# Seventeen weight slots of the Conformer's first product as three matmuls of split parts

## The chip, the cores and the metric

The kernel runs on one core of one Trainium2 chip. The metric is the device time of one execution in microseconds, less is better. Before the change it is 2429.86 us, the median of three runs (2427.54 to 2431.71).

## The reference

Two transformer-like blocks in fp32 follow each other for one sequence of 256 tokens of width 2048. The change lies in the first mixer, the Conformer's convolution, and its first product `h @ w_in`:

```python
def conformer_conv(h, w_in, b_in, dw, dw_b, ln_g, ln_b, w_out, b_out):
    u = h @ w_in + b_in
    val, gate = jnp.split(u, 2, axis=-1)
    u = val * jax.nn.sigmoid(gate)
    u = causal_dwconv(u, dw) + dw_b
    u = jax.nn.silu(layernorm(u, ln_g, ln_b))
    return u @ w_out + b_out
```

h is the normed input (256 x 2048), w_in is 2048 x 4096, and the convolution has 31 taps per channel. Behind it come a squared-relu MLP, a second block (gated delta rule and block attention, cross attention to a memory of 256 rows, a gated FFN) and a last norm. The keys and values of that memory are computed early, right behind the Conformer's first product.

## The kernel before

Activations lie transposed: 128 channels on the partitions, 16 channel tiles, 256 tokens along the free axis. All weights stream from DRAM in slots of 128x1024 fp32 (two channel tiles of 512 columns), one after another in one list, into a ring of four raw buffers `w_raw`. SyncE issues the loads (`sp_load`, L472).

There are two ways to multiply. From the product behind the layer norm on, fp32 is emulated: ScalarE rounds a slot to its high part in fp32r (`act_hi`, L499), VectorE subtracts it from the raw slot to get the low part (`dve_lo`, L508), and TensorE adds hi x hi, hi x lo and lo x hi (`pe_product`, L524, with its matmuls at L553). Before that, in the first 80 slots, it is plain fp32 straight from the raw buffer (`pe_plain_product`, L558): 64 slots of `cc_in` (eight products b = 0 to 7 of eight slots each; a product gives 256 gate and 256 value channels) and 8 slots each of the memory's keys and values. Each plain fp32 matmul shows as two records in the trace.

While TensorE runs product b+1, ScalarE takes the sigmoid of the gates of b (L1065), VectorE multiplies the values with it (glu, L1205) and convolves: for each of two channel tiles of a b a first tap (L1162) and 30 more (L1165), each waiting for the one before it on its tile. Two PSUM accumulators alternate between the products, so product b+2 waits for the glu of b. The glu has three buffers, the gate two. The mean of the layer norm is a set of small matmuls over the convolved tiles (`add_to_mean`, L947); its last part stands on TensorE between keys and values and waits for the last tap. GpSimd clears a few columns at the start and then has nothing to do until the second block.

Each engine has its own program in a fixed order, written out by hand. A helper calls `act_hi` and `dve_lo` once for each slot that TensorE passes, four slots ahead; at the last slot of a product the gates (ScalarE) or the glu (VectorE) stand in front of that call. Other short work (the memory norm's root, the convolution's steps) is put between slots as threads that advance one step per slot.

The first four split slots (80 to 83) are loaded into buffers of their own, `w_first`, that lie over `w_lo`, while slots 64 to 67 are being requested. `w_hi` lies over `mem_in`, the memory's rows.

Of the kernel before, what the change touches and what calls it, by code (L numbers as in the profile page):

```python
# [7 lines left out]
F32 = mybir.dt.float32  # L8
# [5 lines left out]
P = 128  # L14
T = 256
# [188 lines left out]
def side_by_side(both):  # L204
    return Operand(both[:, :, 0, :], both[:, :, 1, :], both)
# [31 lines left out]
STRIP = P // CT  # L237
EARLY = KT // SLOT_K * 2
WARM = 5
WIDE_K = SLOT_K * COLS // PAIR  # L240


class Kernel:
# [40 lines left out]
    def buffers(self):  # L284
        self.x = self.sbuf("x_residual", [P, KT, T])
        with ExitStack() as early:
            self.normed = self.sbuf("h_plain", [P, KT, T], F32, early)
        self.h = side_by_side(self.sbuf("h_operand", [P, KT, 2, T], F32R))
        self.mem_k = self.sbuf("mem_k", [P, NX, T])
        self.mem_v = self.sbuf("mem_v", [P, TT, NX * HD])  # L290
# [18 lines left out]
        with ExitStack() as first:  # L309
            sb = lambda name, shape, dt=F32: self.sbuf(name, shape, dt, first)  # L310
            with ExitStack() as early:
                self.mem_scaled, self.squares = (self.sbuf(n, [P, KT, T], F32, early) for n in ("mem_scaled", "first_squares"))
            with ExitStack() as early:
                self.sbuf("below_conv_hi", [P, KT, T], F32R, early)
                conv_hi = self.sbuf("conv_hi", [P, KT, T], F32R, early)
            hidden = sb("mlp_hidden", [P, KT, 2, T], F32R)
            self.u = sb("conv_out", [P, KT, T])
            self.gate_buf = [sb(f"gate{i}", [P, PT, T]) for i in range(2)]
            self.glu_buf = [sb(f"glu{i}", [P, PT, CONV_K - 1 + T]) for i in range(3)]
            self.mean, self.mem_col = sb("mean", [P, T]), sb("mem_column", [P, TT])  # L320
            self.conv_operand = Operand(conv_hi, sb("conv_lo", [P, KT, T], F32R))
        first, second = (b.rearrange("p k t -> p (k t)") for b in self.tmp_buf)
        self.hot, self.neg, self.rel = first[0:BUCKETS, 0:BIAS_W], second[0:NM, 0:BIAS_W], second[0:BUCKETS, COLS:COLS + NM]
        self.inputs = [self.sbuf(f"heads{g}", [P, 4, CT, T]) for g in range(2)]
# [58 lines left out]
    def plan(self):  # L383
        d = self.dram
        self.parts, self.slots, self.on_pool, self.order = [], {}, [], {}

        def product(key, name, col, pool, k0=0, n=D):
            first = len(self.parts)
            for r in range(k0, k0 + n, SLOT_K * P):
                self.parts.append([d[name][r:r + SLOT_K * P, col:col + COLS].rearrange("(k p) n -> p k n", p=P)])  # L390
            self.slots[key] = range(first, len(self.parts))
            self.on_pool += [pool and i % pool == 0 for i in self.slots[key]]

        def wide(key, name, col, k0=0, n=D, in_turn=False):
            steps, rows = [], range(k0, k0 + n, WIDE_K * P)
            for s, half in [(s, half) for s in range(len(rows)) for half in range(2)] if in_turn else [
                    (s, half) for half in range(2) for s in range(len(rows))]:
                steps.append((half, s, len(self.parts)))
                c = col + half * PAIR
                self.parts.append([d[name][rows[s]:rows[s] + WIDE_K * P, c:c + PAIR].rearrange("(k p) n -> p k n", p=P)])  # L400
                self.on_pool.append(False)
            self.order[key] = [(half, s, i, s == len(rows) - 1) for half, s, i in steps]

        for b in range(D // PAIR):
            first = len(self.parts)
            for r in range(0, D, SLOT_K * P):
                w = d["cc_w_in"][r:r + SLOT_K * P, :].rearrange("(k p) n -> p k n", p=P)
                self.parts.append([w[:, :, D + b * PAIR:D + (b + 1) * PAIR], w[:, :, b * PAIR:(b + 1) * PAIR]])
            self.slots["cc_in", b] = range(first, len(self.parts))
            self.on_pool += [False] * len(self.slots["cc_in", b])  # L410
        product(("keys",), "w_xkv_2", 0, 0)
        product(("values",), "w_xkv_2", COLS, 0)
        self.n_plain = len(self.parts)
        self.early = range(self.n_plain, self.n_plain + SPLIT)
        for b in range(CT):
            product(("cc_out", b), "cc_w_out", b * COLS, 0)
        for kind, c in up_down(N_MLP):
            if kind == "up":
                for b in range(MLP_CHUNK // COLS):
                    wide(("w1", c, b), "mlp_w1", c * MLP_CHUNK + b * COLS, in_turn=c == b == 0)  # L420
            else:
                for b in range(CT):
                    wide(("w2", c, b), "mlp_w2", b * COLS, c * MLP_CHUNK, MLP_CHUNK)
        for g in range(2):
            for part in range(3):
                product(("w_in", part, g), "w_in_2", part * GW + g * COLS, 0)
        for b in MOBA_BLOCKS:
            product(("moba", b), "w_in_2", 4 * GW + 2 * NG + b * COLS, 0)
        for g in range(2):
            product(("w_in", 3, g), "w_in_2", 3 * GW + g * COLS, 0)  # L430
        for half, b in W_OUT_ORDER:
            product(("w_out", half, b), "w_out_2", b * COLS, 0, half * GW, GW)
        wide(("xq",), "w_xq_2", 0)
        for b, half in XO_ORDER:
            product(("xo", b, half), "w_xo_2", b * COLS, 0, half * PAIR, PAIR)
        for kind, c in FFN_ORDER:
            if kind == "up":
                wide(("gate", c), "w_gate_2", c * COLS, in_turn=c == 0)
                wide(("up", c), "w_up_2", c * COLS)
            else:  # L440
                for b in range(CT):
                    wide(("ffn_down", c, b), "w_down_2", b * COLS, c * 2 * COLS, len(chunks_of(c)) * COLS)
        self.n_slots = len(self.parts)

    def lo_done(self, i):
        return (self.pool_done if self.on_pool[i] else self.dve_done).at("w_lo", i)


def spread_row(row, n):
    return row.unsqueeze(1).broadcast_to([P, n, T])  # L450
# [14 lines left out]
def cut(t):  # L465
    return slice(t * P, (t + 1) * P)
# [5 lines left out]
def sp_load(k, sp, i):  # L472
    if i >= k.n_slots:
        return
    if i in k.early:
        return
    if i >= RAW:
        if i - RAW < k.n_plain:
            sp.wait_ge(*k.pe_done.at("used", i - RAW))
        elif i - RAW in k.early:  # L480
            sp.wait_ge(*k.pe_done.at("used", i - 2 * RAW))
        else:
            sp.wait_ge(*k.lo_done(i - RAW))
    parts = k.parts[i]
    w = k.w_raw_wide[i % RAW] if parts[0].shape[1] == WIDE_K else k.w_raw[i % RAW]
    width = w.shape[2] // len(parts)
    for n, part in enumerate(parts):
        sp.dma_start(w[:, :, n * width:(n + 1) * width], part).then_inc(*k.w_landed[i % RAW].mark(i))


def sp_load_early(k, sp, i):
    sp.dma_start(k.w_first[i % SPLIT], k.parts[i][0]).then_inc(*k.w_early[i % SPLIT].mark(i))


# [2 lines left out]


def act_hi(k, act, i):  # L499
    if i >= k.n_slots or i < k.n_plain:  # L500
        return
    act.wait_ge(*(k.w_early[i % SPLIT].at(i) if i in k.early else k.w_landed[i % RAW].at(i)))
    if i >= k.n_plain + SPLIT:
        act.wait_ge(*k.pe_done.at("used", i - SPLIT))
    act.activation(k.w_hi[i % SPLIT], raw_of(k, i), ACT.Copy).then_inc(*k.act_done.mark("w_hi", i))  # L505


def dve_lo(k, dve, i):  # L508
    if i >= k.n_slots or i < k.n_plain or k.on_pool[i]:
        return  # L510
    dve.wait_ge(*k.act_done.at("w_hi", i))
    dve.tensor_tensor(k.w_lo[i % SPLIT], raw_of(k, i), k.w_hi[i % SPLIT].bitcast(F32), ALU.subtract).then_inc(  # L512
        *k.dve_done.mark("w_lo", i))


def pool_lo(k, pool, i):
# [43 lines left out]
def pe_plain_product(k, pe, key, x, ready, tokens_out=False, every=CT):  # L560
    psum, free = k.acc.take(key)
    for f in free:
        pe.wait_ge(*f)
    for s, i in enumerate(k.slots[key]):
        w = k.w_raw[i % RAW]
        pe.wait_ge(*k.w_landed[i % RAW].at(i))
        for part in range(TT if tokens_out else CT):
# [13 lines left out]
        if i == k.slots[key][-1]:  # L581
            k.pe_done.note(*key)
        k.pe_beside.step()


def pe_wide_product(k, pe, key, x, ready, k_tiles=range(KT), every=CT):
# [301 lines left out]
def pool_conformer(k, pool):  # L888
    for i, v in enumerate([1e-6, 1e-5, 128e-6]):
        pool.memset(k.eps[:, i:i + 1], v).then_inc(*k.pool_done.mark("eps"))  # L890
    for buf in k.glu_buf:
        pool.memset(buf[:, :, 0:CONV_K - 1], 0.0).then_inc(*k.pool_done.mark("glu padded"))


def pe_sum_of_squares(k, pe, norm, n_before):
# [104 lines left out]
def act_conformer(k, act):  # L1000
# [66 lines left out]
    for b in range(D // PAIR):  # L1067
        act_product(k, act, ("cc_in", b), lambda: gates(b))
        if b == 0:
            k.act_beside.start(mem_norm())  # L1070
        if b == 5:
            act.wait_ge(*k.dve_done.at("bias rows"))
# [54 lines left out]
def dve_conformer(k, dve):  # L1127
# [26 lines left out]
    def convolve(b):  # L1154
        src = k.glu.at(b)
        dve.wait_ge(*k.dve_done.at("glu", b))
        for j in range(CONV_K):
            for t in range(PT):
                n = b * PT + t
                out, tap, w = k.u[:, n, :], src[:, t, j:j + T], k.col("cc_dw", n * CONV_K + j)  # L1160
                if j == 0:
                    dve.tensor_scalar(out, tap, w, k.col("cc_dw_b", n), ALU.mult, ALU.add).then_inc(*k.dve_done.mark("tap", t, b, j))  # L1162
                else:
                    dve.wait_ge(*k.dve_done.at("tap", t, b, j - 1))
                    dve.scalar_tensor_tensor(out=out, in0=tap, scalar=w, in1=out, op0=ALU.mult, op1=ALU.add).then_inc(  # L1165
# [1824 lines left out]
```

## Time and profile before

| | |
|---|---|
| median of three runs | 2429.86 us (2427.54 to 2431.71) |
| span of the profiled execution | 2427.0 us, 2.9 us under the median |
| TensorE busy | 2395.6 us, 99% |
| VectorE busy | 1658.4 us, 68% |
| ScalarE busy | 1122.0 us, 46% |
| GpSimd busy | 59.5 us, 2% |
| traffic with HBM | 176 GB/s over the span |
| end of the eight first products | 230.8 us |
| end of keys, and of values | 259.3 us, 288.9 us |

The span goes from the first to the last instruction of one profiled execution; the time that this execution took as a whole is not given beside it. Busy shares are averages over stages that differ much. A matmul's duration reaches over the start of the next, so durations don't add up: the distance from start to start is what one costs.

### The profile page before, as it was taken

The numbers are of one execution on the slowest core, as the hardware profiler recorded it, in microseconds if no ns is written. First come the engines' busy times: TensorE is split into PE (matmuls) and PEld (weight loads), VectorE is DVE, ScalarE is ACT, GpSimd is POOL, SyncE is SP. The second block draws the span as 40 slices with busy tenths as digits, with TensorE's granted clock in tenths as the row PEclk, the third lists the DMA queues.
The fourth block names the chain that finished last, engine by engine and source line by source line (L and its number), as shares of the span: only waits on it lengthen the run. The fifth ranks groups of instructions, "written<-read, shape, count | busy, mean of one in ns | idle before, by whom it ended". The sixth has DMA issues, their size and how long they took to land. (4 is left out here: it accounts for less than half of the span.)

```text
span 2427.0 us, 39495 instructions
## 1 busy us (share of the span) xinstructions
PE 2395.6 (99%) x16354; PEld 2126.6 (88%) x16354; DVE 1658.4 (68%) x2310; ACT 1122.0 (46%) x1510; POOL 59.5 (2%) x47
## 2 busy tenths in 40 slices
PE   9999999999999999999999999999999999999998
PEld 8888699888888888889997997998888888888886
DVE  5999756666666666678766455567766767667677
ACT  4000445544544544555637356556544444444444
POOL 0000000000000000000000000000100101000000
PEclk9999999999999999999999999999999999999999
DMA  7446456666666666655444455454666666666663
GB/s 248 152 148 208 146 179 196 191 190 191 190 185 193 190 188 192 190 183 164 141 126 123 123 165 147 157 190 150 191 191 184 194 187 189 189 187 191 186 192 125
DMA packets 379762, 427.96 MB, mean 176 GB/s; under 512 B 16537, under 2 KB 328129, under 8 KB 379585
## 3 DMA queue, kind: packets, MB, share of 16 engines
q1 hardware_dynamic: 374464, 421.58, 56.4%
q10 hardware_dynamic: 5120, 3.86, 0.5%
q8 instruction: 131, 2.15, 0.4%
q14 instruction: 47, 0.38, 0.0%
HBM read 423.27 MB, written 3.67 MB: 176 GB/s over the span
## 5 line engine op out<-in xcount | busy, mean ns | idle before, releaser
L512 DVE TENSOR_TENSOR w_lo<-w_raw,w_hi 128x1024 fp32r<-128x1024 f32 x708 | 868.4, 1229 | 543.8 <-ACT w_hi L505 543.1
L505 ACT ACTIVATE w_hi<-w_raw 128x1024 fp32r<-128x1024 f32 x708 | 747.4, 1058 | 817.9 <-PE product L606 578.6
L604 PE MATMUL product<-h_operand,w_hi 128*128 128x512 f32 x2496 | 867.6, 393 | 0.8 <-DVE x_residual L808 0.8
L606 PE MATMUL product<-h_operand,w_lo 128*128 128x256 f32 x2496 | 696.7, 279 | 0.0
L604 PEld LDWEIGHTS product<-h_operand,w_hi 128*128 128x128 f32 x2496 | 467.8, 187 | 105.9 <-DVE x_residual L808 1.1
L606 PEld LDWEIGHTS product<-h_operand,w_lo 128*128 128x128 f32 x2496 | 471.5, 189 | 0.1
L604 PE MATMUL product<-mlp_hidden,w_hi 128*128 128x512 f32 x1024 | 355.3, 394 | 0.0
L606 PE MATMUL product<-mlp_hidden,w_lo 128*128 128x256 f32 x1024 | 284.0, 277 | 0.0
L604 PE MATMUL product<-mid_operand,w_hi 128*128 128x512 f32 x704 | 248.9, 397 | 0.0
L553 PE MATMUL product<-h_operand,w_hi 128*128 128x256 f32 x1280 | 239.2, 288 | 0.3 <-DVE w_lo L512 0.3
L604 PEld LDWEIGHTS product<-mlp_hidden,w_hi 128*128 128x128 f32 x1024 | 192.3, 188 | 44.7
L578 PE MATMUL product<-h_plain,w_raw 128*128 128x256 f32 x1024 | 222.7, 380 | 0.5 <-DMA w_raw<-in_cc_w_in 0.5
L578 PEld LDWEIGHTS product<-h_plain,w_raw 128*128 128x128 f32 x1024 | 194.5, 190 | 28.5 <-DMA w_raw<-in_cc_w_in 1.3
L553 PEld LDWEIGHTS product<-h_operand,w_hi 128*128 128x128 f32 x1280 | 200.3, 193 | 4.0 <-issue 1.1
L606 PE MATMUL product<-mid_operand,w_lo 128*128 128x256 f32 x704 | 198.4, 282 | 0.0
L606 PEld LDWEIGHTS product<-mlp_hidden,w_lo 128*128 128x128 f32 x1024 | 192.4, 188 | 0.0
L1165 DVE SCALAR_TENSOR_TENSOR conv_out<-glu,feature_columns,conv_out 128x256 f32<-128x256 f32 x480 | 190.8, 474 | 0.0
L661 DVE TENSOR_TENSOR x_residual<-x_residual,product 128x512 f32<-128x512 f32 x224 | 153.8, 687 | 43.2 <-PE product L606 39.4
L553 PE MATMUL product<-h_operand,w_lo 128*128 128x256 f32 x640 | 181.7, 284 | 0.0
L604 PEld LDWEIGHTS product<-mid_operand,w_hi 128*128 128x128 f32 x704 | 132.2, 188 | 32.4
L606 PEld LDWEIGHTS product<-mid_operand,w_lo 128*128 128x128 f32 x704 | 133.2, 189 | 0.0
L553 PEld LDWEIGHTS product<-h_operand,w_lo 128*128 128x128 f32 x640 | 123.4, 193 | 0.0
(333 smaller groups left out, 2242.3 us busy)
## 6 DMA issues: line engine op xcount, KB each, us to landing
w_raw<-in_mlp_w SPq DMA_DIRECT2D x256, 512.0 KB, 3.9
w_raw<-in_w_in SPq DMA_DIRECT2D x112, 512.0 KB, 3.7
w_raw<-in_w_gate SPq DMA_DIRECT2D x88, 512.0 KB, 3.6
w_raw<-in_w_up SPq DMA_DIRECT2D x88, 512.0 KB, 4.1
w_raw<-in_w_down SPq DMA_DIRECT2D x88, 512.0 KB, 4.5
w_raw<-in_cc_w_in SPq DMA_DIRECT2D x128, 256.0 KB, 2.9
w_raw<-in_w_out SPq DMA_DIRECT2D x32, 512.0 KB, 3.7
w_raw<-in_cc_w_out SPq DMA_DIRECT2D x28, 512.0 KB, 4.6
```

Of the source, the lines that this page charges most:

```text
L505: act.activation(k.w_hi[i % SPLIT], raw_of(k, i), ACT.Copy).then_inc(*k.act_done.mark("w_hi", i))
L512: dve.tensor_tensor(k.w_lo[i % SPLIT], raw_of(k, i), k.w_hi[i % SPLIT].bitcast(F32), ALU.subtract).then_inc(*k.dve_done.mark("w_lo", i))
L553: done = pe.matmul(out, stationary, moving, start=first and opens, stop=final, skip_group_check=True)
L578: done = pe.matmul(psum[:, part * T:(part + 1) * T], w[:, kk, cut(part)], x[:, kt, :], start=first and part % 2 == 0, stop=final, skip_gro ...
L604: pe.matmul(out, hi[:, kk, n], x.both[:, kt].rearrange("p a t -> p (a t)"), start=s == 0 and kk == 0, stop=False, skip_group_check=True)
L606: done = pe.matmul(out[:, 0:T], lo[:, kk, n], x.hi[:, kt, :], start=False, stop=last and kk == WIDE_K - 1, skip_group_check=True)
L661: dve.tensor_tensor(x, x, row, ALU.add).then_inc(*k.dve_done.mark("added", *key, half))
L1165: dve.scalar_tensor_tensor(out=out, in0=tap, scalar=w, in1=out, op0=ALU.mult, op1=ALU.add).then_inc(*k.dve_done.mark("tap", t, b, j))
```

## The change

Slots 1, 4 and 6 of the products b = 2 to 7 are taken from the plain path, except slot 62, which a range at the end of the plan clears again: slots 17, 20, 22, 25, 28, 30, 33, 36, 38, 41, 44, 46, 49, 52, 54, 57 and 60. Each gets a high part by ScalarE and a low part by GpSimd, in the rings `w_hi` and `w_lo` that are otherwise unused at that time, and 24 matmuls in place of the 8 plain ones. The activations are split once: high part by ScalarE after the gates of b=0, low part by GpSimd into the buffer of `conv_lo`. The raw buffer of a split slot is free for the next load when GpSimd has subtracted. The first tap of the convolution becomes a scalar_tensor_tensor with the bias column broadcast.

```diff
+SPLIT_FROM, SPLIT_STEPS = 2, (1, 4, 6)
...
-            self.on_pool += [False] * len(self.slots["cc_in", b])
+            self.on_pool += [s in SPLIT_STEPS and b >= SPLIT_FROM for s in range(len(self.slots["cc_in", b]))]
...
+        for i in range(self.n_plain - EARLY - RAW + 1, self.n_plain):
+            self.on_pool[i] = False
+        self.in_parts = [i for i in range(self.n_plain) if self.on_pool[i]]
...
+    def split_of(self, i):
+        n = self.in_parts.index(i)
+        return self.w_hi[n % SPLIT], self.w_lo[n % SPLIT], self.in_parts[n - SPLIT] if n >= SPLIT else None
...
-        if i - RAW < k.n_plain:
+        if i - RAW in k.in_parts:
+            sp.wait_ge(*k.lo_done(i - RAW))
+        elif i - RAW < k.n_plain:
             sp.wait_ge(*k.pe_done.at("used", i - RAW))
...
 def sp_load_early(k, sp, i):
+    sp.wait_ge(*k.pe_done.at("used", k.in_parts[-1]))
...
 def act_hi(k, act, i):
+    if i in k.in_parts:
+        hi, _, before = k.split_of(i)
+        act.wait_ge(*k.w_landed[i % RAW].at(i))
+        act.wait_ge(*(k.act_done.at("squares", "mem_norm", CT - 1) if before is None else k.pe_done.at("used", before)))
+        act.activation(hi, k.w_raw[i % RAW], ACT.Copy).then_inc(*k.act_done.mark("w_hi", i))
...
+    if i in k.early:
+        act.wait_ge(*k.pe_done.at("used", k.in_parts[-1]))
...
+def pool_lo_of_plain(k, pool, i):
+    hi, lo, before = k.split_of(i)
+    pool.wait_ge(*k.act_done.at("w_hi", i))
+    if before is not None:
+        pool.wait_ge(*k.pe_done.at("used", before))
+    pool.tensor_tensor(lo, k.w_raw[i % RAW], hi.bitcast(F32), ALU.subtract).then_inc(*k.pool_done.mark("w_lo", i))
...
+def pe_slot_in_parts(k, pe, psum, s, i):
...
+    pe.wait_ge(*k.pool_done.at("normed lo", s * SLOT_K // CT))
+    pe.wait_ge(*k.act_done.at("w_hi", i))
+    for part, kk in tiles:
+        add(hi, k.normed_hi, part, kk)
+        add(hi, k.normed_lo, part, kk)
+    pe.wait_ge(*k.lo_done(i))
+    for part, kk in tiles:
+        done = add(lo, k.normed_hi, part, kk)
+    return done
...
+    for g in range(CT):
+        part = slice(g * CT, (g + 1) * CT)
+        pool.wait_ge(*k.act_done.at("normed hi", g))
+        pool.tensor_tensor(k.normed_lo[:, part, :], k.normed[:, part, :], k.normed_hi[:, part, :].bitcast(F32),
+                           ALU.subtract).then_inc(*k.pool_done.mark("normed lo", g))
+    for i in k.in_parts:
+        pool_lo_of_plain(k, pool, i)
...
+            for g in range(CT):
+                act.wait_ge(*k.dve_done.at("normed", g))
+                act.activation(k.normed_hi[:, g * CT:(g + 1) * CT, :], k.normed[:, g * CT:(g + 1) * CT, :], ACT.Copy).then_inc(
+                    *k.act_done.mark("normed hi", g))
...
-                    dve.tensor_scalar(out, tap, w, k.col("cc_dw_b", n), ALU.mult, ALU.add).then_inc(*k.dve_done.mark("tap", t, b, j))
+                    dve.scalar_tensor_tensor(out=out, in0=tap, scalar=w, in1=k.col("cc_dw_b", n).broadcast_to([P, T]), op0=ALU.mult,
+                                             op1=ALU.add).then_inc(*k.dve_done.mark("tap", t, b, j))
```

## Rows read from the trace of the kernel before

**Rows 1.** The page: busy time, and the tenths in 40 slices of 60.7 us.
```profile
PE 2395.6 (99%) x16354; PEld 2126.6 (88%) x16354; DVE 1658.4 (68%) x2310; ACT 1122.0 (46%) x1510; POOL 59.5 (2%) x47
...
PE   9999999999999999999999999999999999999998
...
DVE  5999756666666666678766455567766767667677
```

**Rows 2.** Timeline of TensorE: start, duration, line, operation, out<-in, count, idle before.
```profile
72.71 55.42 PE L578 MATMUL product<-h_plain,w_raw 128*128 128x256 f32 x256
127.96 0.38 PE L931 MATMUL small<-masks,rows 128*128 128x128 f32 x2
...
259.28 0.64 PE L952 MATMUL small<-conv_out,masks 128*32 128x256 f32 x8
```

**Rows 3.** Timeline of ScalarE, the gates of b=1.
```profile
62.12 0.84 ACT L1065 ACTIVATE gate<-product,feature_columns 128x256 f32<-128x256 f32 x2 [21.94 <-PE product L578]
```

**Rows 4.** Timeline of VectorE, 70 to 258 us, and the page's row of its taps.
```profile
70.42 0.87 DVE L1205 SCALAR_TENSOR_TENSOR glu<-product,feature_columns,gate 128x256 f32<-128x256 f32 x2
71.33 0.73 DVE L1162 TENSOR_SCALAR conv_out<-glu,feature_columns 128x256 f32<-128x256 f32 x2
71.98 23.83 DVE L1165 SCALAR_TENSOR_TENSOR conv_out<-glu,feature_columns,conv_out 128x256 f32<-128x256 f32 x60
95.74 0.86 DVE L1205 SCALAR_TENSOR_TENSOR glu<-product,feature_columns,gate 128x256 f32<-128x256 f32 x2
...
122.61 0.86 DVE L1205 SCALAR_TENSOR_TENSOR glu<-product,feature_columns,gate 128x256 f32<-128x256 f32 x2
...
175.98 0.88 DVE L1205 SCALAR_TENSOR_TENSOR glu<-product,feature_columns,gate 128x256 f32<-128x256 f32 x2 [2.21 <-ACT gate L1065]
...
203.61 0.88 DVE L1205 SCALAR_TENSOR_TENSOR glu<-product,feature_columns,gate 128x256 f32<-128x256 f32 x2 [2.23 <-ACT gate L1065]
...
232.00 0.88 DVE L1205 SCALAR_TENSOR_TENSOR glu<-product,feature_columns,gate 128x256 f32<-128x256 f32 x2 [2.99 <-ACT gate L1065]
...
233.56 23.83 DVE L1165 SCALAR_TENSOR_TENSOR conv_out<-glu,feature_columns,conv_out 128x256 f32<-128x256 f32 x60
...
L1165 DVE SCALAR_TENSOR_TENSOR conv_out<-glu,feature_columns,conv_out 128x256 f32<-128x256 f32 x480 | 190.8, 474 | 0.0
```

**Rows 5.** Timeline of TensorE, the first product behind the layer norm.
```profile
288.35 0.68 PE L553 MATMUL product<-conv_hi,w_hi 128*128 128x256 f32 x1
288.87 0.28 PE L553 MATMUL product<-conv_lo,w_hi 128*128 128x256 f32 x1
...
309.01 0.28 PE L553 MATMUL product<-conv_hi,w_lo 128*128 128x256 f32 x1
```

**Rows 6.** ScalarE's line L505, its timeline, the page's DMA issues, a window of 217 us.
```profile
L505 ACT ACTIVATE w_hi<-w_raw x708: 1037/1061/1240, 293.4 to 2401.1; 128x1024 fp32r<-128x1024 f32 x177
...
36.92 1.04 ACT L1015 ACTIVATE first_squares<-mem_in 128x1024 f32<-128x1024 f32 x1
...
w_raw<-in_cc_w_in SPq DMA_DIRECT2D x128, 256.0 KB, 2.9
...
40.00:257.00 217.00, 217.00 (x1019) 188.83 (x1018) 208.79 (x519) 13.15 (x23) 0.00 (x0) 1.00 0.52 166
```

**Rows 7.** Timelines of GpSimd and VectorE where both have work, and GpSimd alone.
```profile
1744.20 2.27 POOL L2875 TENSOR_TENSOR heads<-heads,rows 128x512 f32<-128x512 f32 x1 [30.72 <-ACT heads L2714]
...
1744.09 1.22 DVE L512 TENSOR_TENSOR w_lo<-w_raw,w_hi 128x1024 fp32r<-128x1024 f32 x1
1745.23 1.72 DVE L2793 TENSOR_SCALAR heads<-heads,feature_columns 128x256 f32<-128x256 f32 x2
...
1755.35 2.26 POOL L2875 TENSOR_TENSOR heads<-heads,rows 128x512 f32<-128x512 f32 x1 [8.88 <-ACT heads L2714]
...
1757.08 1.62 DVE L512 TENSOR_TENSOR w_lo<-w_raw,w_hi 128x1024 fp32r<-128x1024 f32 x1 [0.61 <-ACT w_hi L505]
...
1709.15 1.30 POOL L2875 TENSOR_TENSOR heads<-heads,rows 128x512 f32<-128x512 f32 x1 [52.09 <-ACT heads L2714]
...
1341.68 0.74 POOL L2051 TENSOR_TENSOR squares<-squares,masks 128x256 f32<-128x256 f32 x1 [10.69 <-PE small L1680]
```

**Rows 8.** Timeline of VectorE, the first low part of the layer norm's output.
```profile
280.41 0.69 DVE L1258 TENSOR_TENSOR conv_lo<-conv_out,conv_hi 128x512 fp32r<-128x512 f32 x1
```

**Rows 9.** TensorE's restart, then windows: PE, PEld, DVE, ACT, POOL busy, PEclk, DMA share, GB/s.
```profile
1517.29 1.08 PE L2069 MATMUL small<-masks,heads 128*128 128x128 f32 x4 [3.14 <-DVE heads L2202]
...
1518.00:1519.00 1.00, 1.00 (x7) 1.00 (x5) 0.27 (x1) 0.59 (x1) 0.00 (x0) 0.50 0.00 0
...
1520.00:1521.00 1.00, 1.00 (x6) 0.80 (x5) 0.00 (x0) 1.00 (x1) 0.00 (x0) 0.89 0.86 295
```

More of the change, by code:

```diff
@@ L287, in buffers @@
             self.normed = self.sbuf("h_plain", [P, KT, T], F32, early)
+            self.normed_hi = self.sbuf("h_plain_hi", [P, KT, T], F32R, early)
         self.h = side_by_side(self.sbuf("h_operand", [P, KT, 2, T], F32R))
@@ L320, in buffers @@
             self.mean, self.mem_col = sb("mean", [P, T]), sb("mem_column", [P, TT])
-            self.conv_operand = Operand(conv_hi, sb("conv_lo", [P, KT, T], F32R))
+            self.normed_lo = sb("conv_lo", [P, KT, T], F32R)
+            self.conv_operand = Operand(conv_hi, self.normed_lo)
         first, second = (b.rearrange("p k t -> p (k t)") for b in self.tmp_buf)
@@ L564, in pe_plain_product @@
     for s, i in enumerate(k.slots[key]):
+        if i in k.in_parts:
+            done = pe_slot_in_parts(k, pe, psum, s, i)
+            done.then_inc(*k.pe_done.mark("used", i))
+            k.pe_beside.step()
+            continue
         w = k.w_raw[i % RAW]
@@ L583, in pe_plain_product, with add @@
         k.pe_beside.step()
+def pe_slot_in_parts(k, pe, psum, s, i):
+    hi, lo, _ = k.split_of(i)
+    tiles = [(part, kk) for part in range(CT) for kk in range(SLOT_K)]
+    def add(w, x, part, kk):
+        return pe.matmul(psum[:, part * T:(part + 1) * T], w[:, kk, cut(part)], x[:, s * SLOT_K + kk, :], start=False, stop=False,
+                         skip_group_check=True)
+    pe.wait_ge(*k.pool_done.at("normed lo", s * SLOT_K // CT))
[7 more added lines that the diff above has]
+    return done
 def pe_wide_product(k, pe, key, x, ready, k_tiles=range(KT), every=CT):
```

## The prediction

> **What bounds the kernel now.** I read the page first. TensorE is busy for 99% of the span and VectorE for 68%, but slices 2 to 4 of the tenths (61 to 243 us) show both at 9: in the Conformer's first product VectorE is as full as TensorE [rows 1]. So I asked for the timeline of each engine in the first 300 us. TensorE goes from plain fp32 matmul to plain fp32 matmul without a gap; between 72.71 us and 127.96 us it runs 256 records, which are 16 slots, so a slot takes 55.25 / 16 = 3.45 us and a product b of eight slots 27.6 us [rows 2]. VectorE convolves behind it. A tap goes every 23.83 / 60 = 0.397 us, and a whole b takes 95.74 - 70.42 = 25.3 us. VectorE starts late (glu of b=1 at 70.42, though its gate was done at 62.96 [rows 3]), catches up by about 2.3 us per b, and first waits at b=5. It waits 2.21, 2.23 and 2.99 us in b=5, 6 and 7, 7.4 us together, and that is all the spare time that it has until the last tap at 233.56 + 23.83 = 257.4 us [rows 4]. TensorE needs that last tap at 259.28 us, for the mean of the layer norm [rows 2]. Two clocks thus run to that point, and VectorE's is late by nature: 1.9 us of slack behind it, 7.4 us in it.
>
> **What TensorE gains.** Slots 1, 4 and 6 of b = 2 to 7 are split, except slot 62, which the range at the end of the plan clears: 6 x 3 - 1 = 17. A plain slot is 8 tiles of two records, 3.45 us. A split one is 24 matmuls of 256 columns. The order hi with hi, hi with lo, lo with hi is in the trace as the product behind the layer norm, where 172 starts lie between 288.87 and 309.01 us, 0.1171 us each [rows 5], so 24 of them take 2.81 us. A slot saves 0.64 us, 17 save 10.9 us, all on TensorE's own path. TensorE alone would be at the mean at 248.4 instead of 259.3 us.
>
> **What feeds the split.** ScalarE gets 17 conversions of weights and four of the activations, 1.06 us each, 22.3 us [rows 6], beside the 13.2 us that it is busy in the 217 us between 40 and 257 us. A raw slot is asked for when the slot four before it is done, lands 2.9 us later [rows 6], and TensorE arrives three slots, 10.4 us, after the request. 10.4 - 2.9 - 1.1 leaves 6.4 us for GpSimd's part, more than twice what it takes below, so I cost ScalarE and the new waits of SyncE at nothing. If this cover is gone (slot 4 of a b, whose conversion is queued behind the gates of the b before, and these behind VectorE's glu of two b before), TensorE waits for as long as ScalarE was held; queued there too are the root of the memory norm and the later conversions. Gates of b need glu of b-2, as TensorE's accumulator of b does, so the hold adds nothing to that wait. SyncE's load into a raw buffer of a split slot waits for GpSimd's subtraction and not for TensorE: earlier, nothing lost. The early loads behind the last split slot (60) stand in a queue that has already waited for slot 60: nothing. w_hi lies over the memory rows; ScalarE has finished their squares at 37.96 us [rows 6], well before slot 17.
>
> **What GpSimd takes from VectorE.** GpSimd gets 4 + 17 = 21 subtractions of 128x1024, and VectorE's taps, each reading glu and conv_out from SBUF, run beside all of them. The trace has no such pair, so I take the nearest rows [rows 7]. At 1744.20 a GpSimd multiply of 128x512 begins 0.11 us after the start of a VectorE subtraction, which ends at 1745.31; it ends at 1746.47, 1.16 us after that subtraction. Alone the same multiply takes 1.30 us, so it did nothing until VectorE had finished. VectorE's next pair, two tensor_scalar of 128x256, was ready at 1745.23 and took 1.72 us; a like pair with GpSimd idle takes 0.73 us [rows 4]. VectorE lost 0.99 of the 1.16 us. At 1757.08 a weight subtraction falls into the rest of a GpSimd multiply (over at 1757.61), takes 1.62 us, not 1.22, and ends 1.09 us behind the multiply: 0.13 us of its start were hidden. So the two engines exclude each other for a whole instruction, and GpSimd came first at the change of instruction even where VectorE had the next one ready. For 1024 elements: alone 128x256 takes 0.74 us, 128x512 1.30 us, so 2.19 ns an element, and the hold is 1.16 + 512 x 2.19 ns = 2.28 us, the loss 2.28 - 0.15 = 2.13 us. The bounds for one subtraction: 0, if taps don't collide; 2.5 us, if nothing of its start is hidden. A gain is excluded, since nothing is taken off VectorE. I take 2.13, because the weight subtraction (two SBUF inputs, fp32, one element per cycle) is the same kind of reader as a tap. 21 x 2.13 = 44.7 us.
>
> The Trainium skill, "SBUF — State Buffer", section "SBUF: two separate sides", says the port pair shared by VectorE and GpSimd is an exclusive lock, which a VectorE operation with two SBUF inputs takes too against a GpSimd operation that reads SBUF, and the loser blocks fully. By that rule taps collide like the weight subtraction, which no row here shows for a tap; if only VectorE's faster modes took the lock, the sum would be the first rival's. The same skill, "GPSIMD Engine Reference", section "Performance versus the Vector engine", gives 4497 ns for 2048 elements; by it, as an estimate, the hold is 2.25 us and the sum 0.6 us lower.
>
> **VectorE's own edit.** The first tap becomes a scalar_tensor_tensor. A pair of the old ones is followed after 0.65 us (71.33 to 71.98), of the new after 2 x 0.397 = 0.79 us [rows 4]: 0.15 us for each of 8 b, 1.2 us.
>
> **The sum.** VectorE never waits now: last tap at 257.4 - 7.4 + 44.7 + 1.2 = 295.9 us. On the way TensorE is held too. Products alternate between two accumulators, so product b+2 starts only when glu of b is done. Glu of b=3, at 122.61 before, comes after some ten subtractions at about 144 us, when TensorE (114 us at the end of b=3) has just finished or is about to finish b=4; from there TensorE follows VectorE at 25.5 + 3 x 2.1 = about 32 us per b, so each b has idle stretches of some 6 us. These are inside VectorE's time. It ends the keys near 275 us and waits for the last tap until 295.9 instead of 259.3: +36.6 us. Behind it nothing is tight: in the layer norm the first low part is ready at 281.1 for TensorE's 288.35 [rows 5, 8], and both move together. A wait of some 20 us brings TensorE's clock down. The only long waits of the trace show it: idle from 1514.1 to 1517.3, granted clock 0.50 (1.2 GHz of 2.4) until 1520, 0.89 in the next slice [rows 9]; some 3.3 us at half speed lose 1.7 us. Only the last wait's counts, as the others lie in VectorE's shadow. 2427.0 + 36.6 + 1.7 = 2465.3 us of span. The span is 2.9 us under the median of 2429.86; with the same 2.9 the median becomes 2468.2 us.
>
> **Rivals.**
> First, faster: the taps don't collide, or hardly. For it: no row shows a tap beside GpSimd being held. Against: 1744.20 and 1757.08 [rows 7]. VectorE then ends at 257.4 - 7.4 + 1.2 = 251.2 us, later than TensorE's 248.4, so of the 10.9 us only 259.3 - 251.2 = 8.1 are gained: 2421.8 us. This is the other sign, and it turns at (8.1 / 21) = 0.39 us lost per subtraction: below this the kernel is faster, above it slower.
> Second, worse: taps follow each other so closely that VectorE keeps the port, and GpSimd gets it only where VectorE has a gap or reads PSUM (glu). For it: taps overlap by 0.08 us (0.474 long, 0.397 apart [rows 4]), and the only pair that showed who comes next was not two taps. Against: there too the next instruction had started before the other ended, and GpSimd got in. Then slot 17 waits for five subtractions until VectorE runs dry at 96 us, ends at about 106, and b=2 at 125 instead of 88; each further b waits for VectorE at its slot 4 and takes 40 us. Last tap: 125 + 5 x 40 + 25 = 350 us, +91: about 2523 us.
> Third: the subtractions collide, but in part (handover cheap, a third to two thirds of the hold lost): 0.8 to 1.5 us each, last tap at 268 to 283, 2439 to 2455 us.
>
> **Chances and range.** Forecast 0.67; taps not colliding 0.17; in part 0.09; GpSimd starved 0.05; anything else 0.02. The forecast's own range is 2459 to 2478 us: 1.9 to 2.5 us for each subtraction gives -5 to +8, TensorE's clock and a delayed row of the memory norm the rest. Two in ten must not be left out, so the range goes down to the first rival: 2420 to 2478. A change of 0.2%, 4.9 us, is about what can be told from none. Faster: the first rival and a little of the third at its cheap end, 0.18. Same: 0.04, losses near 0.39 us. Slower: 0.78.
>
> **What would show it.** TensorE: the split slots at 0.117 us per matmul, waits for VectorE's glu from b=5 on, and one of some 20 us before the strips of the mean. VectorE: no idle time at the glu of b=5 to 7, taps beside GpSimd of 2.5 us and more, their mean raised from 474 to about 570 ns. GpSimd: 21 subtractions of 2.3 to 2.7 us. ScalarE: 17 more conversions and no wait of TensorE for them. I am wrong if taps beside GpSimd keep their 474 ns, or if TensorE's longest new wait is for GpSimd.

## The result: 2493.0 us, 2.6% slower

The changed kernel takes 2492.97 us (median of four runs, 2491.29 to 2493.68) against 2430.30 us before; the ratio is 1.0259, 95% interval 1.0240 to 1.0278. Slower was forecast, but at 2468 us with 2478 as the upper end. The measured rise of 62.7 us is 1.6 times the forecast's 38.3.

First the page of the changed kernel: busy time, then the tenths of its 40 slices (62.3 us each).

```profile
PE 2401.1 (96%) x16490; PEld 2138.9 (86%) x16490; DVE 1686.0 (68%) x2310; ACT 1143.6 (46%) x1531; POOL 198.4 (8%) x68
...
PE   9886899999999999999999999899999999999998
...
DVE  5996676666666666678766455467776766767677
...
POOL 2556200000000000000000000000010100000000
PEclk9987899999999999999999999999999999999999
```

Beside [rows 1], TensorE has lost its nines in slices 2 to 5, and VectorE its nine in slice 4 (in 5 it goes from 7 to 6): both engines that filled this stage now idle in it. TensorE's granted clock falls in slices 3 to 5. GpSimd is busy for 198 us, not the 108 that its 59.5 and 21 subtractions of 2.3 us make. The rest of the span looks as before.

Who TensorE waited for from 60 to 290 us (us in all, times, longest):

```profile
PE product L624 <- POOL w_lo L541: 54.5, 7, 13.7
PE product L624 <- ACT w_hi L517: 3.3, 1, 3.3
```

L624 is the split slot's matmuls, L541 GpSimd's subtraction. Before the change TensorE waited for nothing here. Now 57.8 us are waits for a split slot's parts, nearly all for the low part of the weights. So GpSimd's timeline comes next. In it the duration of an instruction counts from its issue, and a wait for the SBUF port that GpSimd shares with VectorE is inside it:

```profile
41.10 9.83 POOL L947 TENSOR_TENSOR conv_lo<-h_plain,h_plain_hi 128x1024 fp32r<-128x1024 f32 x4 [39.97 <-ACT h_plain_hi L1130]
59.86 6.95 POOL L541 TENSOR_TENSOR w_lo<-w_raw,w_hi 128x1024 fp32r<-128x1024 f32 x1 [8.93 <-ACT w_hi L517]
70.16 2.34 POOL L541 TENSOR_TENSOR w_lo<-w_raw,w_hi 128x1024 fp32r<-128x1024 f32 x1 [3.34 <-ACT w_hi L517]
77.72 7.58 POOL L541 TENSOR_TENSOR w_lo<-w_raw,w_hi 128x1024 fp32r<-128x1024 f32 x1 [5.23 <-ACT w_hi L517]
86.72 2.66 POOL L541 TENSOR_TENSOR w_lo<-w_raw,w_hi 128x1024 fp32r<-128x1024 f32 x1 [1.42 <-ACT w_hi L517]
99.40 17.15 POOL L541 TENSOR_TENSOR w_lo<-w_raw,w_hi 128x1024 fp32r<-128x1024 f32 x2 [10.02 <-ACT w_hi L517]
...
155.84 20.33 POOL L541 TENSOR_TENSOR w_lo<-w_raw,w_hi 128x1024 fp32r<-128x1024 f32 x2 [8.43 <-ACT w_hi L517]
185.42 19.77 POOL L541 TENSOR_TENSOR w_lo<-w_raw,w_hi 128x1024 fp32r<-128x1024 f32 x2 [9.25 <-ACT w_hi L517]
217.40 22.84 POOL L541 TENSOR_TENSOR w_lo<-w_raw,w_hi 128x1024 fp32r<-128x1024 f32 x2 [12.21 <-ACT w_hi L517]
250.03 2.35 POOL L541 TENSOR_TENSOR w_lo<-w_raw,w_hi 128x1024 fp32r<-128x1024 f32 x1 [9.79 <-ACT w_hi L517]
268.92 11.58 POOL L541 TENSOR_TENSOR w_lo<-w_raw,w_hi 128x1024 fp32r<-128x1024 f32 x1 [16.54 <-ACT w_hi L517]
```

Let in at once, a subtraction takes 2.34 or 2.35 us (70.16, 250.03). Of the rows with two, the first alone takes 14.6 (99.40), 17.8 (155.84), 17.4 (185.42) and 20.5 us (217.40). The reader should compare their ends with VectorE's timeline, which answers to [rows 4]:

```profile
142.62 0.87 DVE L1268 SCALAR_TENSOR_TENSOR glu<-product,feature_columns,gate 128x256 f32<-128x256 f32 x2
143.53 4.17 DVE L1224 SCALAR_TENSOR_TENSOR conv_out<-glu,feature_columns 128x256 f32<-128x256 f32 x2
147.62 23.84 DVE L1228 SCALAR_TENSOR_TENSOR conv_out<-glu,feature_columns,conv_out 128x256 f32<-128x256 f32 x60
171.38 0.87 DVE L1268 SCALAR_TENSOR_TENSOR glu<-product,feature_columns,gate 128x256 f32<-128x256 f32 x2
172.28 4.17 DVE L1224 SCALAR_TENSOR_TENSOR conv_out<-glu,feature_columns 128x256 f32<-128x256 f32 x2
...
210.17 0.88 DVE L1268 SCALAR_TENSOR_TENSOR glu<-product,feature_columns,gate 128x256 f32<-128x256 f32 x2 [9.51 <-ACT gate L1123]
211.08 0.88 DVE L1224 SCALAR_TENSOR_TENSOR conv_out<-glu,feature_columns 128x256 f32<-128x256 f32 x2
211.88 23.83 DVE L1228 SCALAR_TENSOR_TENSOR conv_out<-glu,feature_columns,conv_out 128x256 f32<-128x256 f32 x60
252.75 0.88 DVE L1268 SCALAR_TENSOR_TENSOR glu<-product,feature_columns,gate 128x256 f32<-128x256 f32 x2 [17.03 <-ACT gate L1123]
...
295.14 0.88 DVE L1268 SCALAR_TENSOR_TENSOR glu<-product,feature_columns,gate 128x256 f32<-128x256 f32 x2 [16.84 <-ACT gate L1123]
296.05 0.88 DVE L1224 SCALAR_TENSOR_TENSOR conv_out<-glu,feature_columns 128x256 f32<-128x256 f32 x2
296.85 23.84 DVE L1228 SCALAR_TENSOR_TENSOR conv_out<-glu,feature_columns,conv_out 128x256 f32<-128x256 f32 x60
```

Sixty taps from 147.62 take 23.84 us, the 23.83 of [rows 4] and not a hold among them, though GpSimd asked at 155.84. It got the port at the glu of 171.38, and both its subtractions were over by 176.17: the two first taps behind that glu took 4.17 us instead of 0.88. TensorE had been waiting for the first subtraction. In b=5 to 7 the glus stand 42.6 and 42.4 us apart. VectorE finishes its taps, GpSimd gets in, TensorE finishes the product, and only then may the next glu begin; so VectorE waits 17 us for TensorE after TensorE has waited for VectorE's taps to end.

Both engines' accounts close. VectorE's last tap ends at 320.7 us, before at 257.4: 63.3 later. Its idle time grew from 7.4 to 43.4 us, +36.0; the other 27.3 are 1.2 of its own edit and 26.1 of holds. TensorE reaches the mean at 322.43 instead of 259.28 [rows 2]: +63.1, of which 57.8 are waits and -10.9 the saving. I put the rest, 16.2 us, down to its clock, which each of the long waits brings down. In windows of 1 us from 60 to 330, TensorE's busy time times the missing share of the granted clock comes to 14.5 us, so some 2 us of it stay unexplained. The split slot at 269 us starts its matmuls 0.21 us apart, the one at 256 us 0.12 us:

```profile
256.00 0.28 PE L624 MATMUL product<-h_plain_hi,w_hi 128*128 128x256 f32 x1
256.11 0.28 PE L624 MATMUL product<-conv_lo,w_hi 128*128 128x256 f32 x1
...
269.55 0.41 PE L624 MATMUL product<-h_plain_hi,w_hi 128*128 128x256 f32 x1
269.76 0.41 PE L624 MATMUL product<-conv_lo,w_hi 128*128 128x256 f32 x1
```

### The profile page after: what moved, and what is told of

Its sections match the earlier page's. It is cut to its first block and busy times, and to the rows that moved or that the text cites. A ratio compares the mean times of both kernels' runs of the same rounds, so it can differ in the third digit from the quotient of the medians.

```text
span 2490.0 us, 39849 instructions
## 1 busy us (share of the span) xinstructions
PE 2401.1 (96%) x16490; PEld 2138.9 (86%) x16490; DVE 1686.0 (68%) x2310; ACT 1143.6 (46%) x1531; POOL 198.4 (8%) x68
## 5 line engine op out<-in xcount | busy, mean ns | idle before, releaser
L657 PEld LDWEIGHTS product<-h_operand,w_lo 128*128 128x128 f32 x2496 | 472.5, 189 | 0.1
L655 PEld LDWEIGHTS product<-mlp_hidden,w_hi 128*128 128x128 f32 x1024 | 191.7, 187 | 41.5
L1228 DVE SCALAR_TENSOR_TENSOR conv_out<-glu,feature_columns,conv_out 128x256 f32<-128x256 f32 x480 | 199.8, 494 | 0.0
L611 PE MATMUL product<-h_plain,w_raw 128*128 128x256 f32 x752 | 173.6, 391 | 0.5 <-DMA w_raw<-in_cc_w_in 0.5
L611 PEld LDWEIGHTS product<-h_plain,w_raw 128*128 128x128 f32 x752 | 147.1, 198 | 22.8 <-DMA w_raw<-in_cc_w_in 1.3
L541 POOL TENSOR_TENSOR w_lo<-w_raw,w_hi 128x1024 fp32r<-128x1024 f32 x17 | 129.1, 7604 | 100.5 <-ACT w_hi L517 100.5
```

The source lines that it names most:

```text
L541: pool.tensor_tensor(lo, k.w_raw[i % RAW], hi.bitcast(F32), ALU.subtract).then_inc(*k.pool_done.mark("w_lo", i))
L611: done = pe.matmul(psum[:, part * T:(part + 1) * T], w[:, kk, cut(part)], x[:, kt, :], start=first and part % 2 == 0, stop=final, skip_gro ...
L655: pe.matmul(out, hi[:, kk, n], x.both[:, kt].rearrange("p a t -> p (a t)"), start=s == 0 and kk == 0, stop=False, skip_group_check=True)
L657: done = pe.matmul(out[:, 0:T], lo[:, kk, n], x.hi[:, kt, :], start=False, stop=last and kk == WIDE_K - 1, skip_group_check=True)
```

## The experiments

Theory A: a subtraction that asks for the port while taps run is not let in until the taps pause; TensorE waits for it, then VectorE for TensorE. Theory B: the holds of VectorE are the cost and are dearer than forecast. Each experiment edits the changed kernel. The ratios are against the kernel before on the same chip.

**A pause in the taps.**
```diff
             if j % 4 == 3:
+                dve.wait_ge(*k.dve_done.at("tap", PT - 1, b, j))
                 yield
```


> VectorE waits for its last tap after every fourth pair of taps, so that there is an instant without a tap every 3.3 us; everything else is as in the changed kernel. Theory A (a subtraction that asks for the port while taps run is not let in until the taps pause; TensorE waits for it, then VectorE for TensorE): TensorE's waits for GpSimd, 54.5 us, go almost wholly, VectorE keeps its loss of about 2.1 us for each of 21 subtractions, 2458 to 2474 us. Theory B (the 2493 us come from what VectorE is held, a hold is dearer than forecast): no gain, 2493 to 2500 us, since more subtractions now cut into taps.

2475.7 us, ratio 1.0194 (1.0175 to 1.0213): 17 us faster than the changed kernel by the medians, 2 us above A's range (2458 to 2474), and far from B. Here is GpSimd, then VectorE's last b, then TensorE's waits:

```profile
59.81 2.37 POOL L541 TENSOR_TENSOR w_lo<-w_raw,w_hi 128x1024 fp32r<-128x1024 f32 x1 [8.81 <-ACT w_hi L517]
70.23 2.44 POOL L541 TENSOR_TENSOR w_lo<-w_raw,w_hi 128x1024 fp32r<-128x1024 f32 x1 [8.05 <-ACT w_hi L517]
...
198.55 3.82 POOL L541 TENSOR_TENSOR w_lo<-w_raw,w_hi 128x1024 fp32r<-128x1024 f32 x1 [15.98 <-ACT w_hi L517]
...
275.00 24.71 DVE L1228 SCALAR_TENSOR_TENSOR conv_out<-glu,feature_columns,conv_out 128x256 f32<-128x256 f32 x60
...
PE small L1010 <- DVE conv_out L1228: 23.3, 1, 23.3
PE product L611 <- DVE glu L1269: 18.4, 4, 7.2
```

All 17 subtractions now take 2.34 to 3.82 us, and TensorE waits for none of them. It waits as the forecast had it: some 5 us for the glu in the later b and 23.3 us for the last tap. That tap ends at 299.7. The pause itself costs 24.71 - 23.83 = 0.88 us in a b, 7.0 in eight; without it the end would be at 292.7, where the forecast has 295.9. That is 41.5 us above the 251.2 without GpSimd, 1.98 us for each of 21.

**The low parts by VectorE.** All 21 subtractions move to VectorE, as steps between taps. Shown is the part for the weights.
```diff
...
 def dve_lo(k, dve, i):
+    if i in k.in_parts:
+        hi, lo, before = k.split_of(i)
+        dve.wait_ge(*k.act_done.at("w_hi", i))
+        if before is not None:
+            dve.wait_ge(*k.pe_done.at("used", before))
+        dve.tensor_tensor(lo, k.w_raw[i % RAW], hi.bitcast(F32), ALU.subtract).then_inc(*k.dve_done.mark("w_lo", i))
...
```


> All 21 subtractions by VectorE instead of GpSimd, as steps between its taps; TensorE as in the changed kernel. Theory A and B alike: no port to share, VectorE pays 21 x 1.14 us = 24 us and has 7.4 us idle, last tap at 257.4 - 7.4 + 1.2 + 24 = 275 us, 2444 to 2450 us, if TensorE's low parts come in time. Rival: VectorE is so late with its steps that TensorE waits at split slots in turn: over 2455 us.

2446.6 us, ratio 1.0081 (1.0053 to 1.0109). The last tap ends at 275.6, the sum said 275. TensorE waits 13.1 us for low parts in small pieces; these lie inside VectorE's time. The same split without the shared port costs 46 us less than the changed kernel, and still more than no split.

**No subtraction at all.** The split slots' matmuls read the high parts twice, low parts are left out, GpSimd has nothing to do, and the next load into a split slot's raw buffer waits for ScalarE's conversion alone.
```diff
...
-        add(hi, k.normed_lo, part, kk)
-    pe.wait_ge(*k.lo_done(i))
+        add(hi, k.normed_hi, part, kk)
     for part, kk in tiles:
-        done = add(lo, k.normed_hi, part, kk)
+        done = add(hi, k.normed_hi, part, kk)
...
```


> No subtraction at all: the 24 matmuls of a split slot take the high parts in place of the low ones, so the low parts of weights and activations are left out; ScalarE's conversions stay. Shows what TensorE's edit brings without GpSimd. The forecast's terms: 8 us faster than before, 2420 to 2424 us, VectorE the last at the mean. Rival (ScalarE's conversions or the loads' new waits cost TensorE): 2427 us and more.

2423.9 us (ten runs), ratio 0.9984 (0.9974 to 0.9995). The interval is narrow enough for a gain, a small one. The last tap is over at 250.9 (forecast 251.2), and TensorE is at the mean 7.3 us earlier than before:

```profile
227.10 23.83 DVE L1220 SCALAR_TENSOR_TENSOR conv_out<-glu,feature_columns,conv_out 128x256 f32<-128x256 f32 x60
...
251.97 0.64 PE L1002 MATMUL small<-conv_out,masks 128*32 128x256 f32 x8
```

This is the ceiling of the change: even with low parts for nothing, 17 split slots bring some 5 us by the medians (2428.8 to 2423.9).

**The port's price alone.** TensorE multiplies plain in all slots; 21 subtractions run on GpSimd at their times, and nobody waits for them until the layer norm.
```diff
...
-        if i in k.in_parts:
-            done = pe_slot_in_parts(k, pe, psum, s, i)
...
-    pool.tensor_tensor(lo, k.w_raw[i % RAW], hi.bitcast(F32), ALU.subtract).then_inc(*k.pool_done.mark("w_lo", i))
+    pool.tensor_tensor(k.normed_lo[:, part, :], k.normed[:, part, :], k.normed_hi[:, part, :].bitcast(F32),
+                       ALU.subtract).then_inc(*k.pool_done.mark("w_lo", i))
...
```


> TensorE multiplies plain fp32 in all 64 slots; ScalarE's conversions and 21 subtractions of 128x1024 on GpSimd run at their places, but nobody waits for a subtraction before the layer norm (the 17 of the weights are made from the activations instead, which no product reads). Price of the port for VectorE alone. Theory A: the port costs VectorE up to 21 x 2.13 = 45 us, of which it has 7.4 idle, so 2455 to 2468 us; the rest up to 2493 is TensorE's wait. Theory B: 2485 us and more. If taps win the port and GpSimd mostly runs at a glu for nothing: under 2445 us.

2455.9 us, ratio 1.0111 (1.0094 to 1.0128), the lower end of A's range. GpSimd's queue piles up behind the taps, VectorE never idles, and its last tap ends at 288.1:

```profile
157.25 23.76 POOL L542 TENSOR_TENSOR conv_lo<-h_plain,h_plain_hi 128x1024 fp32r<-128x1024 f32 x3 [7.88 <-ACT w_hi L517]
...
264.24 23.83 DVE L1226 SCALAR_TENSOR_TENSOR conv_out<-glu,feature_columns,conv_out 128x256 f32<-128x256 f32 x60
```

288.1 - 251.2 = 36.9 us for 21 holds, 1.76 each. The port alone thus accounts for 27 us over the kernel before (2455.9 against 2428.8). The changed kernel loses another 37 us although TensorE has less to do in it: that part needs TensorE waiting for GpSimd.

**Which slots are split.** Six slots each time, ten subtractions, as `SPLIT_STEPS = 2, (1,)` and `2, (4,)`. Theory C: the loss goes by the number of subtractions.

> Only slot 1 of b = 2 to 7 is split (6 slots, 10 subtractions in all). Theory A (a subtraction that meets running taps waits for the next glu): slot 1's weights are converted in the last slots of the product before, shortly ahead of the glu of that product, which lets GpSimd in; TensorE hardly waits, VectorE pays 10 x 1.8 to 2.1 us of which 7.4 are idle, 2436 to 2445 us. Theory C (the loss goes by the number of subtractions, 62.7 / 21 = 3 us each, wherever they stand): 10 x 3 = 30 us, 2459 us.

> Only slot 4 of b = 2 to 7 is split (6 slots, 10 subtractions, as many as with slot 1 alone). Theory A: slot 4's weights are ready in slot 2, just behind the glu of the product before, so the subtraction waits until VectorE has run out of taps and TensorE waits with it, most in the later b; 2475 to 2500 us with a third of the split slots. Theory C: as with slot 1 alone, 2459 us.

Slot 1: 2445.3 us, ratio 1.0073 (1.0052 to 1.0094). Slot 4: 2456.8 us, ratio 1.0116 (1.0091 to 1.0141). The order is A's, but for slot 4 the number is C's, and A's 2475 to 2500 is missed. For slot 1 A's range (2436 to 2445) is met at its upper end. The traces show TensorE's waits for GpSimd, of slot 1 and then of slot 4:

```profile
109.01 2.07 PE L624 MATMUL product<-h_plain_hi,w_lo 128*128 128x256 f32 x8 [13.79 <-POOL w_lo L541]
```

```profile
81.46 2.07 PE L624 MATMUL product<-h_plain_hi,w_lo 128*128 128x256 f32 x8 [3.31 <-POOL w_lo L541]
...
242.20 2.08 PE L624 MATMUL product<-h_plain_hi,w_lo 128*128 128x256 f32 x8 [19.12 <-POOL w_lo L541]
```

The error was to fix the place of the glu in TensorE's product. VectorE was late in both, and its lateness moved: with slot 4 GpSimd asked 2 to 4 us ahead of a glu four times (at 102.70, glu at 105.77), once 9 us ahead (at 70.11, glu at 79.13), and missed it once, the last time (asked at 220.88, glu at 214.43); with slot 1 it missed once, early (asked at 87.46, glu at 81.22). A miss cost TensorE 13.8 and 19.1 us, the request 9 us ahead 3.3, the others nothing. The traced execution of slot 4 took 2464.1 us, the longest of its four, so its miss may be larger than in the others (2453.8 to 2457.6). With three split slots in a b TensorE waited seven times. Phase, the distance from the request to the next glu, fits all of these waits; its outcome can't be told from the slot's number.

**The old first tap back.**
```diff
-                    dve.scalar_tensor_tensor(out=out, in0=tap, scalar=w, in1=k.col("cc_dw_b", n).broadcast_to([P, T]), op0=ALU.mult,
-                                             op1=ALU.add).then_inc(*k.dve_done.mark("tap", t, b, j))
+                    dve.tensor_scalar(out, tap, w, k.col("cc_dw_b", n), ALU.mult, ALU.add).then_inc(*k.dve_done.mark("tap", t, b, j))
```


> The changed kernel with the old first tap (tensor_scalar, one tensor input). Theory A: GpSimd gets in because the glu in front of the first taps reads PSUM; the form of the first tap matters by its own 0.15 us a b at most, 2488 to 2496 us. Rival (the new form, with two SBUF inputs, shuts GpSimd out or lets it in where the old would not): more than 5 us away from 2493.

2493.4 us, ratio 1.0268 (1.0238 to 1.0298): the form of the first tap decides nothing.

## Why the prediction was wrong, point by point

The step that failed is this one of "What GpSimd takes from VectorE": "GpSimd came first at the change of instruction even where VectorE had the next one ready." In [rows 7] the next one was a tensor_scalar, with one tensor input; behind a tap comes a tap, with two. (That the number of inputs is what matters is not shown; see the end of this section.) Among taps GpSimd is mostly shut out, for up to 18 us (asked at 217.40, taps over at 235.71). The cover of 6.4 us, worked out in "What feeds the split", had been measured against a subtraction that starts when it asks, and so that step fell with the first. The second rival described what happened (the port only at a gap or at the glu, 40 us for each b that waits; measured 42), and I had given it 0.05. Its price of 2523 us was too high: the first four subtractions (asked from 41.10 us on, 0.09 us ahead of a first tap) were all over by 50.9 us, and b=2 and b=3 took VectorE 31 and 29 us from glu to glu, not 40.

Right, by the runs:
- The bound. VectorE's 7.4 us and TensorE's 1.9 are all the slack; without low parts TensorE is at the mean 7.3 us earlier, where the first rival had 8.1 and TensorE alone would have had 10.9.
- A split slot. 0.118 us from matmul to matmul at full clock, 2.81 forecast for 24.
- The exclusion. Taps and subtractions exclude each other for a whole instruction; one hold costs 1.98 us where GpSimd gets in promptly, forecast 2.13. A tap took 2.59 us where GpSimd had asked 0.03 us before it, as the two rows below show. The rule cited from the Trainium skill, "SBUF — State Buffer", section "SBUF: two separate sides", that the loser blocks fully, thus holds for taps too:

```profile
70.16 2.34 POOL L541 TENSOR_TENSOR w_lo<-w_raw,w_hi 128x1024 fp32r<-128x1024 f32 x1 [3.34 <-ACT w_hi L517]
...
70.19 2.59 DVE L1228 SCALAR_TENSOR_TENSOR conv_out<-glu,feature_columns,conv_out 128x256 f32<-128x256 f32 x1
```

- The sum that follows. With a pause in the taps the last tap, less the pause's own price, is at 292.7 for a forecast of 295.9, and TensorE's waits are those foretold.
- VectorE's own edit: first taps 0.80 us apart as a pair (211.08 to 211.88), forecast 0.79.
- ScalarE's conversions cost TensorE next to nothing: one wait of 3.3 us. ScalarE itself had waited for that slot's load: asked for at 255.96, it let the conversion begin only at 267.78, and from 258 to 268 us the DMA engines were busy to 0.85 to 0.91, with the copy of `bias_rows` (1524 KB, issued at 251.86) under way. The run without low parts has such a wait too, 2.3 us at 210.18, as far behind that copy (193.98), so GpSimd is not its cause; no run moved the copy.

Wrong in size: the clock. Forecast was one fall, 1.7 us at the mean, the others covered. There was no wait at the mean, and the falls within the stage cost TensorE 14 to 16 us, in b=5 to 7 uncovered, as VectorE waited for TensorE there.

Wrong in what would show it: no wait of TensorE for the glu occurred. Its longest wait was for GpSimd, which the text had named as a sign of error. The taps' mean rose from 474 to 494 ns only, as most subtractions ran beside a glu and its first taps or an idle VectorE; with the pauses it was 553, for a forecast of about 570.

No version that makes the low parts beat the kernel before. The run without low parts bounds what any number of split slots could bring here at 5 us or so, as VectorE is next in line; the low parts cost more than that wherever they were made.

Open: what exactly lets GpSimd in. GpSimd, waiting since 59.86, came in between these two:

```profile
63.37 1.21 DVE L969 TENSOR_TENSOR first_squares<-first_squares 128x1024 f32<-128x1024 f32 x1
64.61 3.29 DVE L972 TENSOR_TENSOR first_squares<-first_squares 128x1024 f32<-128x1024 f32 x1
```

VectorE was empty for 0.03 us there. Seven changes of instruction without such an instant, each next one begun some 0.08 us before the last was over, had passed it by. That fits, and so does the pause. But at 86.72 it asked 0.02 us after a tap had begun and got in behind that tap, and at 59.86, 0.01 us after another, it did not. And at a glu (171.38) it got in without such an instant. No run separated these.

## What to carry to other kernels

Work given to an idle engine is free only if it shares nothing with the engine that is full; look for a row in which the newcomer meets the same sequence that it will meet (here tap behind tap), not one instruction of that kind. Two questions need separate answers: what does the newcomer cost the full engine, and when does it get its turn; the second turned a loss of 27 us into one of 63. Before making work cheaper on the engine that seems to be the bound, find how far behind it the next engine is: here 9 us, so nothing larger could be won.

## What the runs showed of the hardware that was not expected

- Back-to-back VectorE instructions with two SBUF inputs, each started 0.08 us before the one before it ended, kept a waiting GpSimd subtraction out for up to 18 us (about 46 taps). A single wait on VectorE's last tap, every 3.3 us, let it in each time: no subtraction of a weight slot then lasted over 3.82 us from its issue.
- The instruction that waits shows as a long one: GpSimd's 128x1024 subtraction is 2.34 us when let in at once and up to 20.5 us when not, with no sign of waiting but its length.
- Not everything on VectorE is held by a subtraction beside it. With the pauses, a RECIPROCAL (one input) that began 0.05 us after a subtraction took its usual 1.75 us, and the subtraction its 2.35; in the changed kernel the glu of 171.38, which reads a PSUM accumulator, kept its 0.87 us beside one too. So a subtraction let in at a glu costs VectorE less than one among taps, which fits 1.76 us a hold without pauses against 1.98 with them:

```profile
131.11 2.35 POOL L541 TENSOR_TENSOR w_lo<-w_raw,w_hi 128x1024 fp32r<-128x1024 f32 x1 [16.19 <-ACT w_hi L517]
...
131.16 1.75 DVE L816 RECIPROCAL rows<-rows 128x256 f32<-128x256 f32 x1
```

- TensorE's granted clock was 0.50 (1.2 of 2.4 GHz) after each of seven waits for a split slot's part (2.99 to 13.72 us), for 3 to 6 us from the restart on unless the next wait came first, and 1.00 (2.4 GHz) after the one of 1.36 us. Eight matmuls took 2.08 us after a wait of 2.99 us and 1.22 us after that of 1.36. The windows are of the changed kernel (busy of PE, PEld, DVE, ACT, POOL, then the granted clock):

```profile
85.36 1.22 PE L624 MATMUL product<-h_plain_hi,w_lo 128*128 128x256 f32 x8 [1.36 <-POOL w_lo L541]
...
144.96 2.08 PE L624 MATMUL product<-h_plain_hi,w_lo 128*128 128x256 f32 x8 [2.99 <-POOL w_lo L541]
...
230.00:240.00 10.00, 2.03 (x9) 2.04 (x10) 5.71 (x15) 0.00 (x0) 10.00 (x2) 0.50 0.09 25
240.00:250.00 10.00, 10.00 (x50) 8.81 (x49) 0.00 (x0) 1.06 (x1) 0.24 (x1) 0.81 0.40 125
```
